# Grouped-query attention taken head by head, with the split values as stationary operand and a fixed use of the PSUM banks

## The reference, cut to what matters

```python
def gqa_mixer(q, k, v, q_norm, k_norm, row, col):
    q = rope_2d(rms_norm(q.reshape(B, L, N_Q_HEADS, HEAD_DIM), q_norm), row, col)
    k = rope_2d(rms_norm(k.reshape(B, L, N_KV_HEADS, HEAD_DIM), k_norm), row, col)
    ...
        s = jnp.einsum('bkgqd,bksd->bkgqs', qblk, kt).astype(jnp.float32) * scale
        p = jax.nn.softmax(s, axis=-1).astype(vt.dtype)
        return jnp.einsum('bkgqs,bksd->bkgqd', p, vt)
y = jnp.concatenate([group_rms_norm(y_hy, out_norm_hyena[i], HYENA_GROUPS),
                     group_rms_norm(y_at, out_norm_attn[i], N_Q_HEADS)], axis=-1)
x = x + y @ w_out[i]
```

## Time and profile before

| | |
|---|---|
| median of 3 runs | 804.22 us (802.68 to 804.98) |
| the profiled execution | 803.55 us, its span 801.7 us |
| TensorE busy | 760.3 us (95%) |
| VectorE busy | 605.2 us (75%) |
| ScalarE busy | 458.9 us (57%) |
| GpSimd busy | 73.6 us (9%) |
| the 384 matmuls of `pv`, records added | 106 us |

### The profile page before, as it was taken

How to read it: one execution, slowest core, us unless ns; L and a number is a source line. 1 busy time by engine, 2 the same in 40 slices (tenths; PEclk the granted TensorE clock), 3 DMA queues, 4 the chain that set the end, 5 groups by cost and what they waited for, 6 DMA issues and landing times.

```text
span 801.7 us, 11083 instructions
## 1 busy us (share of the span) xinstructions
PE 760.3 (95%) x3804; PEld 620.6 (77%) x3804; DVE 605.2 (75%) x929; ACT 458.9 (57%) x676; POOL 73.6 (9%) x86
## 2 busy tenths in 40 slices
PE   5899999999999899989897998999999999999994
PEld 3665868788898799978785696888888888888883
DVE  5767483996889778833447468799998999999882
ACT  5942333121243867622359342688877888888773
POOL 0000000000000000000000001112222232322111
PEclk8999999999999999999999998899999999999998
DMA  8730303020130110012221376899999999999841
GB/s 291 290 105 1 91 15 105 27 79 1 53 88 19 48 59 2 2 52 79 79 79 53 139 277 258 336 396 373 360 373 378 376 393 372 376 373 379 337 176 21
DMA packets 28543, 146.54 MB, mean 183 GB/s; under 512 B 4791, under 2 KB 6711, under 8 KB 21976
## 3 DMA queue, kind: packets, MB, share of 16 engines
q1 hardware_dynamic: 23320, 135.53, 44.8%
q0 software_dynamic: 5184, 10.50, 5.0%
HBM read 141.81 MB, written 12.58 MB: 193 GB/s over the span
## 4 chain that ended last, share of the span: by engine, by line
PE 76%; DVE 9%; ACT 7%; DMA 4%; issue 2%; SPq 0%; POOL 0%; ACTq 0%; POOLq 0%; DVEq 0%
PE bank L1912 17%; PE bank L1850 16%; PE bank L2278 10%; PE bank L2280 10%; PE bank L2279 10%; PE bank L1857 3%; PE bank L2273 2%; DMA slot<-in_w_down 2%; PE bank L1924 1%; ACT pr L938 1%; PE bank L2192 1%; PE bank L2190 1%; PE bank L2191 1%; PE bank L2315 1%; DVE w_lo L1108 1%
## 5 line engine op out<-in xcount | busy, mean ns | idle before, releaser
L1769 DVE TENSOR_TENSOR e_lo<-slot,e_hi 128x1024 fp32r<-128x1024 f32 x192 | 221.3, 1218 | 7.7 <-ACT e_hi L988 7.6
L988 ACT ACTIVATE e_hi<-slot 128x1024 fp32r<-128x1024 f32 x192 | 188.0, 1061 | 5.4 <-DMA slot<-in_w_down 3.7
L1108 DVE TENSOR_TENSOR w_lo<-w_raw,w_hi 128x1024 fp32r<-128x1024 f32 x41 | 49.4, 1222 | 75.6 <-ACT w_hi L694 75.5
L694 ACT ACTIVATE w_hi<-w_raw 128x1024 fp32r<-128x1024 f32 x41 | 42.6, 1057 | 101.2 <-DMA w_raw<-in_w_in 63.4
L2278 PE MATMUL bank<-e_hi,hgT_hi 128*128 128x512 f32 x240 | 94.9, 395 | 0.0
L2280 PE MATMUL bank<-e_hi,hgT_lo 128*128 128x512 f32 x240 | 93.6, 390 | 0.0
L2279 PE MATMUL bank<-e_lo,hgT_hi 128*128 128x512 f32 x240 | 93.4, 389 | 0.0
L2280 PEld LDWEIGHTS bank<-e_hi,hgT_lo 128*128 128x128 f32 x240 | 45.1, 188 | 9.6
L2278 PEld LDWEIGHTS bank<-e_hi,hgT_hi 128*128 128x128 f32 x240 | 45.3, 189 | 8.9
L2279 PEld LDWEIGHTS bank<-e_lo,hgT_hi 128*128 128x128 f32 x240 | 45.1, 188 | 8.9
L2278 PE MATMUL bank<-e_hi,gaT_hi 128*128 128x512 f32 x120 | 48.1, 401 | 0.0
(11 more groups left out here) (392 smaller groups left out, 1710.0 us busy)
## 6 DMA issues: line engine op xcount, KB each, us to landing
slot<-in_w_down SPq DMA_DIRECT2D x16, 2048.0 KB, 15.6
slot<-in_w_gate SPq DMA_DIRECT2D x16, 2048.0 KB, 14.7
slot<-in_w_up SPq DMA_DIRECT2D x16, 2048.0 KB, 14.8
w_raw<-in_w_in SPq DMA_DIRECT2D x18, 512.0 KB, 3.6
w_raw<-in_w_out SPq DMA_DIRECT2D x8, 512.0 KB, 3.7
w_raw<-in_w_k_mem SPq DMA_DIRECT2D x4, 512.0 KB, 6.3
x_in<-in_x SPq DMA_DIRECT2D x4, 512.0 KB, 9.3
w_raw<-in_w_v_mem SPq DMA_DIRECT2D x4, 512.0 KB, 5.3
```

What stands on the lines that cost most here:

```text
L694: act.activation(w_hi[ring(m)][:], w_raw[ring(m)][:], ACT.Copy).then_inc(s_wh, 1)
L988: act.activation(e_hi[buffer(b, j)][:], slot[slot_][:, 1024 * part:1024 * (part + 1)], ACT.Copy).then_inc(s_ehi, 1)
L1108: dve.tensor_tensor(w_lo[slot_][:], w_raw[slot_][:], w_hi[slot_][:].bitcast(F32), ALU.subtract)\
L1769: dve.tensor_tensor(e_lo[slot_][:, at_], slot[slot_][:, at_], e_hi[buffer(b, j)][:].bitcast(F32), ALU.subtract)\
```

## The change

The steps run head by head: s = 4h + i. Two query tiles of a head form a pair. `v_split` holds for each key tile the 64 high and the 64 low columns of v side by side, and is now the stationary operand; the transposed probabilities of the pair, 256 columns, move, high part and low part. `pv(j)` runs in every second step with eight such matmuls, into rows 0 to 63 (v high) and 64 to 127 (v low) of bank "O". After four steps a head is complete, transposed: ScalarE copies it (`out_copy`), TensorE multiplies it by a stacked identity (`out_T`, four matmuls of 64 columns, float32), which adds the two halves and turns it back, ScalarE copies the result to `att` (`out_rows`, 256 columns), GpSimd squares it, VectorE sums it. Six banks serve "S" and "PT" alone, bank 6 "O", and bank 7 every other job of the stage in turn. `gqa_max` runs one step further ahead. The squares of the Hyena output, `mk_normed` and the output squares go to GpSimd. The two sums matmuls in each of eight steps become four in each of four; the Hyena norms stand in steps 22, 23, 25 and 26 of VectorE; query and key transposes are spread over later steps; 16 constant products are put before the first ten `pt`. In the diff cut here, column numbers of the small statistics follow the new order of the steps.

```diff
...
-HR_STEP = 19
...
-HR_STEPS = [HR_STEP + 3 * c for c in range(CT)]
+HR_STEPS = [20, 21, 23, 24]
 GATED_STEP = 1
-HN_STEPS = range(GATED_STEP + CT + 1, GATED_STEP + CT + 1 + 2 * TT)
+HN_STEPS = [7, 11, 12, 15]
 MK_STEP = 9
+QT_STEPS = [1, 3, 9, 13, 17, 19]
+KT_STEPS = [5, 8]
+OT_STEPS = [TT * h + 6 for h in range(NQ - 1)]
+FILL = [3, 3, 2, 2] + [1] * 6
...
-    jobs += [("kT", 0), ("kT", 1), ("qT", 0), ("qT", 1), ("qT", 2), ("qT", 3)]
+    jobs += [("kT", 0), ("kT", 1), ("qT", 0), ("qT", 1)]
     n = TT * NQ
     jobs += [("S", s) for s in range(AHEAD)]
     for s in range(-2, n):
-        if s >= 0 and s % NQ == 0:
-            jobs += [("O", s // NQ)]
+        if s >= 0 and s % TT == 1:
+            jobs += [("O", s // TT)]
         if s + 2 + AHEAD < n:
             jobs += [("S", s + 2 + AHEAD)]
         if s + 2 < n:
             jobs += [("PT", s + 2)]
-        if s == -1:
-            jobs += [("kT", 2), ("kT", 3)]
-        if s + 6 < NQ:
-            jobs += [("qT", s + 6)]
+        if s in OT_STEPS:
+            jobs += [("OT", OT_STEPS.index(s))]
+        if s in KT_STEPS:
+            jobs += [("kT", 2 + KT_STEPS.index(s))]
+        if s in QT_STEPS:
+            jobs += [("qT", 2 + QT_STEPS.index(s))]
         if s in HN_STEPS:
             jobs += [("hn", HN_STEPS.index(s))]
         if s in HR_STEPS:
             jobs += [("hr", HR_STEPS.index(s))]
+    jobs += [("OT", NQ - 1)]
...
+        v_split = at("v_split", 192, [P, TT, NKV, 2, HD], F32R)
...
+        pT_hi = at("pT_hi", 56, [P, NPR // 2, 4, 2 * P], F32R)
+        pT_lo = at("pT_lo", 72, [P, NPR // 2, 4, 2 * P], F32R)
...
+        oT = at("oT", 184, [P, 2, T])
+        o_sq = at("o_sq", 188, [P, 2, TT, HD])
+        ident_pair = at("ident_pair", 191, [P, HD])
...
+        tail_s = jobs.index(("yT", 0))
         last_s = max(n for n, j in enumerate(jobs) if j[0] == "PT")
         for n, j in enumerate(jobs):
             if j[0] == "O":
-                b = 6 + j[1] % 2
+                b = 6
+            elif first_s < n < tail_s and j[0] not in ("S", "PT"):
+                number[j] = len(number)
+                b = 7
...
+        def column(s):
+            return NQ * (s % TT) + s // TT
+        def pair_half(buf, s):
+            return buf[:, s // 2 % 2, :, (s % 2) * P:(s % 2 + 1) * P]
+        def out_head(h):
+            return att[:, :, h * HD:(h + 1) * HD]
...
+            pool.wait_ge(s_qinv, 1)
+            pool.tensor_tensor(ident_pair[:], ident[:, 0:HD], ident[:, HD:P], ALU.add).then_inc(s_pair, 1)
+            for c in range(CT):
+                pool.wait_ge(s_z, CT + c + 1)
+                pool.tensor_tensor(y_sq[:, c, :], u[:, c, :], u[:, c, :], ALU.mult).then_inc(s_ysq, 1)
+            def mk_normed(j):
+                pool.wait_ge(s_minv, 1)
+                x3 = mk[:, j, :].rearrange("p (h d) -> p h d", d=MHD)
+                link(pool.tensor_tensor(x3, x3, small[:, 40 + MH * j:44 + MH * j].unsqueeze(2).to_broadcast([P, MH, MHD]), ALU.mult))
+                pool.tensor_tensor(x3, x3, row("gmk").unsqueeze(1).to_broadcast([P, MH, MHD]), ALU.mult).then_inc(s_mkn, 1)
+            def out_square(h):
+                wait_freed(pool, ("OT", h))
+                if h >= 2:
+                    pool.wait_ge(s_oss, h - 1)
+                pool.tensor_tensor(o_sq[:, h % 2], out_head(h), out_head(h), ALU.mult).then_inc(s_osq, 1)
+            out_square(0)
+            mk_normed(0)
+            out_square(1)
+            mk_normed(1)
+            out_square(2)
             pool.wait_ge(s_hrec, 1)
             pool.tensor_copy(inv_wide[:].rearrange("p t c w d -> p (t c w) d"),
                              small[:, 280:312].unsqueeze(2).to_broadcast([P, 8 * TT, HD])).then_inc(s_hwide, 1)
+            for h in range(3, NQ):
...
-            for h in range(1, 4):
-                qT_evac(h)
+            qT_evac(1)
...
+                c0 = column(s)
...
                 if s >= NPR:
-                    act.wait_ge(s_asq, s - NPR + 1)
-                act.activation(pT_hi[:, s % NPR, :], bank(("PT", s))[:], ACT.Copy).then_inc(s_phi, 1)
-            def out_square(i):
-                job = ("O", i)
-                act.wait_ge(s_asq, (i + 1) * NQ)
-                act.activation(o_sq[:, i, :], bank(job)[:], ACT.Square).then_inc(s_osq, 1)
-                free(act.activation(att[:, i, :], bank(job)[:], ACT.Copy), job)
+                    act.wait_ge(s_asq, s // 2 - 1)
+                act.activation(pair_half(pT_hi, s), bank(("PT", s))[:].rearrange("p (k n) -> p k n", k=4), ACT.Copy).then_inc(s_phi, 1)
+            def out_copy(h):
+                act.wait_ge(s_asq, 2 * h + 2)
+                if h >= 2:
+                    wait_filled(act, ("OT", h - 2))
+                free(act.activation(oT[:, h % 2, :], bank(("O", h))[:], ACT.Copy), ("O", h))
+            def out_rows(h):
+                job = ("OT", h)
+                wait_filled(act, job)
+                free(act.activation(out_head(h), bank(job)[:, 0:TT * HD].rearrange("p (i d) -> p i d", i=TT), ACT.Copy), job)
...
-            qT_evac(4)
             for s in range(NSEQ):
                 gqa_pt_hi(s)
                 if s + AHEAD < NSEQ:
                     gqa_exp(s + AHEAD)
-                if s == 0:
-                    kT_evac(2)
-                    kT_evac(3)
-                if s + 5 < NQ:
-                    qT_evac(s + 5)
-                if GATED_STEP < s <= GATED_STEP + CT:
-                    y_square(s - GATED_STEP - 1)
+                if s % TT == 0 and s > 0:
+                    out_copy(s // TT - 1)
+                if s - 1 in OT_STEPS:
+                    out_rows(OT_STEPS.index(s - 1))
+                if s - 1 in KT_STEPS:
+                    kT_evac(2 + KT_STEPS.index(s - 1))
+                if s - 1 in QT_STEPS:
+                    qT_evac(2 + QT_STEPS.index(s - 1))
                 if s == HN_STEPS[-1] + 2:
                     hyena_root()
-                if s in (10, 12, 14):
-                    weight_hi(26 + (s - 10) // 2, 1)
-                if s % NQ == 3 and s > NQ:
-                    out_square(s // NQ - 1)
+                if s in (11, 14, 17):
+                    weight_hi(26 + (s - 11) // 3, 1)
             act.activation(small[:, 398:399], eps, ACT.Sqrt)
-            out_square(TT - 1)
+            out_copy(NQ - 1)
+            out_rows(NQ - 1)
...
-                dve.wait_ge(s_osq, i + 1)
-                return dve.tensor_reduce(small[:, 340 + NQ * i:340 + NQ * (i + 1)], o_sq[:, i, :].rearrange("p (h d) -> p h d", d=HD),
-                                         AX.X, ALU.add)
+                free(dve.tensor_tensor(pair_half(pT_lo, s), bank(job)[:].rearrange("p (k n) -> p k n", k=4),
+                                       pair_half(pT_hi, s).bitcast(F32), ALU.subtract), job)
+            def out_sums(h):
+                dve.wait_ge(s_osq, h + 1)
+                return dve.tensor_reduce(small[:, 340:372].rearrange("p (i h) -> p i h", h=NQ)[:, :, h], o_sq[:, h % 2], AX.X, ALU.add)
...
-            for s in range(AHEAD):
+            for s in range(AHEAD + 1):
                 gqa_max(s)
+            dve.wait_ge(s_hrms, 1)
+            dve.reciprocal(small[:, 40:48], small[:, 40:48]).then_inc(s_minv, 1)
...
-                    gqa_max(s + AHEAD)
+                if s + AHEAD + 1 < NSEQ:
+                    gqa_max(s + AHEAD + 1)
...
-                if MK_STEP <= s < MK_STEP + MT:
-                    mk_normed(s - MK_STEP)
-                if s in (11, 13, 15):
-                    weight_lo(26 + (s - 11) // 2, 1)
-                if s % NQ == 4 and s > NQ:
-                    link(out_sums(s // NQ - 1))
+                if s in (12, 15, 19):
+                    weight_lo(26 + (12, 15, 19).index(s), 1)
+                if s - 3 in OT_STEPS:
+                    out_sums(OT_STEPS.index(s - 3)).then_inc(s_oss, 1)
...
-            link(out_sums(TT - 1))
+            for h in (NQ - 2, NQ - 1):
+                ins = out_sums(h)
+            link(ins)
...
-            for h in range(4):
+            for h in range(2):
                 qT_job(h)
...
-                for m in range(2):
-                    t, c = divmod(2 * n + m, CT)
-                    ins = pe.matmul(bank(job)[:, 2 * m:2 * m + 2], y_sq[:, c, t * P:(t + 1) * P], blk[:, 0::HD], start=True, stop=True)
+                for c in range(CT):
+                    ins = pe.matmul(bank(job)[:, 2 * c:2 * c + 2], y_sq[:, c, n * P:(n + 1) * P], blk[:, 0::HD], start=True, stop=True)
                 done(ins)
...
             def score(s):
-                i, h = s // NQ, s % NQ
+                i, h = s % TT, s // TT
                 job = ("S", s)
                 open_bank(pe, job)
-                if s < NQ:
+                if i == 0:
                     wait_freed(pe, ("qT", h))
-                if s in (0, NQ // 2):
...
             def pt(s):
+                if s < len(FILL):
+                    constant_products(("PT", s), FILL[s])
```

(50 more changed lines are left out.)

40 lines of the change are left out of this document (12 added, 28 removed).

## The result

The changed kernel takes 808.51 us (median of 20 executions, 806.06 to 810.70), the kernel before beside it 804.98. Some executions (one of run 4, the others of the kernel before) are slow ones of 819 to 852 us at a lower mean granted clock, which none of the ratios and not this 804.98 count. The ratio is 1.0038, 95% interval 1.0024 to 1.0053: 3 us slower, where 4 us faster were forecast and 806.5 us was the upper end of the range. The profiled execution took 808.8 us, its span is 806.9 against 801.7.

What follows compares the result with a forecast made beforehand. TensorE, 95% busy, was taken to bound attention, with VectorE and ScalarE close behind. Stretch gains 6.2 and 2.6 less losses 2.5 and 2.9 gave 3.4 us off 803.55, so 800.2 us; range 792 to 806.5.

Steps and rivals of the forecast that it cites:

- a bar of 70% of 39 us at half speed: Attention from 300 us on: a clock fall decides for "slower" only if more than 70% of these 39 us run slow.
- a wait of 2.8 us for the exponential behind the table load: Around step 20: TensorE waits 2.8 us while ScalarE's exponential 20 stands behind root, copies and table loads.
- second bank wait: Steps 20 to 24: TensorE's "hr" transposes wait for bank 7 until VectorE's norms free it; delays of 1.1 and 1.0 us.
- stretch C: Attention from the copy of transposes 20 to the last transposes, PT(31): 27.0 us against 24.5, a loss of 2.5.
- A: Attention up to ScalarE's copy of transposes 10: ends at 282.3 us instead of 288.5, a gain of 6.2.
- B: Attention from the copy of transposes 10 to that of transposes 20: 23.5 us against 26.15, a gain of 2.6.
- D: From the last transposes, PT(31), to the yT transposes: 20.6 us against 17.7, a loss of 2.9.
- Rival 3: Attention from 314.65 us through the first four output tiles: TensorE's clock falls to 1.2 GHz, 8.7 us more, 808.9; chance 0.07.
- GpSimd's hold on VectorE: Steps 2 to 5: VectorE's multiply waits for GpSimd's squares, 2.4 us a step instead of 2.05; costs TensorE 1.5 us.
- bank 7 in it: Between the copy of transposes 20 and PT(31): bank waits of 1.1 and 1.0 us, plus 0.5 for `out_rows` and hand-over.
- The signs to look for: Trace marks: `pv` products 0.12 us apart, GpSimd products near 1.0 and 0.6, held-up multiplies 0.5 to 1, norm waits in steps 21, 24.
- yT at 353.5: End of attention: the yT transposes start at 353.5 us of the span, with the stages after as long as before.

Runs made afterwards that it cites:

- run 4: The kernel before with the products of `pT_hi` with `v_lo` left out of `pv`, 14.3 us less TensorE work; 808.96 us, 1.0053 of the kernel before.
- run 6: The changed kernel with products of constants filling the places where TensorE waited, up to the yT transposes; 802.62 us, 0.9982 of the kernel before.
- Run 8: The changed kernel without its own 16 constant products ahead of the transposes of steps 0 to 9; 807.81 us, 1.0034 of the kernel before.
- run 10: The changed kernel with 18 products of constants ahead of the yT transposes, nothing else; 804.87 us, 1.0003 of the kernel before.

## Why the prediction was wrong

**The step that failed is the clock.** The sum had no term for it: I took 1.00 for the whole stage since the kernel before has 1.00 there, and gave a fall 0.07. The argument for so little was a comparison of busy shares with memory attention, and a bar of 70% of 39 us at half speed. The forecast's own numbers held a warning: a wait of 2.8 us for the exponential behind the table load, where the longest wait of the kernel before from 259 to 340 us is 1.3. Behind it, behind the second bank wait and at yT the clock fell. It cost 30.24 − 27.04 = 3.2 us in stretch C. At yT the transposes took 3.67 − 1.97 = 1.7 us more, of which 1.1 reached the copies behind them (the changed kernel against run 6: 3.31 us at yT, 4.40 at the copy of the memory keys' transposes). Together that is 4.3 us, and the two ratios differ by 0.56%, 4.5 us.

**The clock is about half of the miss.** By the spans, the forecast was 3.4 us earlier and 5.2 later came out, 8.6 apart. The clock is 4.3 of them; A and B are 2.7 together, D gave 0.3 back, and the other 1.9 arise in the experts, which the sum had at nothing.

**Rival 3 came close to the time for a partly wrong reason.** It gave 808.9, and 808.5 was measured. But it had all of C and the first four tiles at half speed, 8.7 us; the two falls in C were some 3.4 us long each (0.72 in a window of 6 us) and cost 4.3 with the restart at yT, and the rest of the miss came from A, B and the experts. So its agreement is luck. That it "decides from where more than 70% of these 39 us run slow" was wrong, because the gain to be used up was smaller than 3.4.

**Stretches A and B were each 1.3 us short.** In A the sum over TensorE was right, partly by luck, and the step behind it wrong. Transposes 10 are issued at 281.71 and take 0.43, so they end at 282.14; the forecast had 282.2. Within it a `pv` takes 1.03 us (266.37 to 267.40) and not 0.96, since its first distance is 0.21; the constant products took 3.9 and not 3.5; TensorE's waits were 1.7 and not 2.4, as GpSimd's hold on VectorE was real, but cost TensorE 0.16 us in a low part and not 1.5. Then I let the copy follow at once. In the trace it starts 1.5 us later: ScalarE stood 1.40 us in `out_copy`(1), which waits for `pv`(3) (281.44 above), and had copy 9, exponential 11 and a key evacuation to do ahead of copy 10. I had charged these late evacuations nothing. Run 8 tells the same, 0.83 us for 3.5 of TensorE's work. In B transposes 10 to 20 are 306.60 − 281.71 = 24.9 us apart where I had 23.5: the waits recorded are 3.9 against 3.4 (the one behind the table load 2.74, forecast 2.8), five `pv` 0.35 more, and some 0.5 us of small distances stay unexplained.

**Stretches C and D were right in sum but for the clock.** C: 27.0 forecast, 27.04 with the clock held, bank 7 in it 2.6 against 2.5. The other terms met the sum by luck: in run 6 maximum 23 starts at 309.19, 0.8 us behind the border and not 2.2; from there to the end of maximum 31 with its multiply (332.96) it is 23.8 us and not 22.7, and from there to PT(31) 2.5 and not 2.1. D: 20.6 against 20.32. The signs to look for were right too: 0.12 us a product, GpSimd 1.04 and 0.61 (1.30 with the spread row as an input), the multiply 0.50, waits on the norm in steps 21 and 24, plus one I had not seen in step 22, out_T(4) behind the same bank (1.80). "A granted clock below 1.00 between 300 and 335" was named as what would be wrong, and came. "yT at 353.5" would have needed the clock and 2 us more.

**What follows yT** was to move along unchanged. The copy of the memory keys' transposes is 3.28 us later than before (399.82 against 396.54): 2.14 at yT and the slow restart. The end is 5.2 later. The other 1.9 us arise among the experts, behind 732 us, where the difference is still 2.0. ScalarE's waits for the transfers of expert weights from 700 us to the end are 13.1 us in sum against 3.7. No run separates this; it stays open.

**What stays open of the clock:** why a fall lasted some 3.4 us in one run and 30.7 in another, what let the clock rise at 323.9 us in run 4, and why it fell behind some waits and not behind others, longer ones among them. It is shown that the falls of attention come behind idle time, and that they go when the idle time is filled.

## What to carry to other kernels

Count TensorE's clock as a term whenever a change gives TensorE slack: taking narrow work away lost more than it gained here (run 4), and the first places to look at are the new waits, at a table load or a shared bank, the short ones too. Where TensorE must wait anyway, products of constants into a bank that is free, a little shorter than the wait, cost nothing that was measured and kept the clock here; check for the clock by filling the time of the work you removed, which parts it from the work itself. And give evacuated extras more than one bank when their reader runs two steps late.

## What the chip showed

The clock goes between 1.00 and 0.50 within one `pv` (0.11 to 0.21 us a product at 293.2 us of run 4) after two waits of 0.36 us. The Trainium skill, TensorE: Matmul & The Clock Gate, section "A second HAM failure mode: psum-queue depth-cycling", describes such a case, short idle times between groups of matmuls that let the clock go back and forth between its two levels. The trace of the changed kernel agrees (0.72, 1.00 and 0.72 in the windows from 306 to 326 us); that of run 4 agrees in the short idle times but not in the back and forth, since the clock stayed at 0.50 for 30.7 us.

The same program gets different clocks in different executions: 0.973 to 0.987 in run 10, with 8 us between the shortest and the longest span. In memory attention the same code has 0.66 from 437 to 447 us in the profile of the kernel before and 1.00 in that of run 6. A single profile is not enough to place a change of 0.3% that touches TensorE's waits.

GpSimd's product of two 128x512 float32 operands takes 1.04 us, of two 128x256 ones 0.61 or 0.62, but 1.35 and 1.15 in two of the changed kernel's. Its effect on VectorE is larger in the trace than on the path: the 128x1 multiply beside it ends when GpSimd does, 1.4 us of delay in stretch A, while TensorE's wait for a low part there is 0.16.
